# Reading the moving columns of two feed-forward projections in pieces, in a two-block transformer kernel

## The chip, the cores and the metric

The kernel runs on one core of a Trainium2 chip. The metric is device time in microseconds (us) of one execution. Inputs, weights and the output are in HBM; everything is float32.

## What is computed

Two transformer blocks over 512 tokens of width 1024. The change touches the feed-forward networks of the second block, which has two layers (`conv_ffn`, with `D_FF` = 2816):

```python
def causal_dwconv(u, w):
    width = w.shape[0]
    s = u.shape[1]
    up = jnp.pad(u, ((0, 0), (width - 1, 0), (0, 0)))
    return sum(up[:, i:i + s] * w[i] for i in range(width))

def conv_ffn(xn, w_up, conv_w, w_down):
    up = xn @ w_up
    a, g = jnp.split(up, 2, axis=-1)
    a = causal_dwconv(a, conv_w)
    return (jax.nn.silu(a) * g) @ w_down
```

and in `second_block`, for both layers: `xn = rmsnorm(x, ffn_norm[l])`, `x = x + conv_ffn(xn, ffn_w_up[l], ffn_conv[l], ffn_w_down[l])`. The first block has a network of the same shape with GELU. So there are three gate-and-value projections (`xn @ w_up`, 1024 to 5632 features): `up0` in the first block, `up1` and `up2` in the second.

## The kernel before

The activations lie transposed: 128 features on the partitions, 512 tokens along the free dimension, so a width of 1024 is a tile of 8 blocks of [128, 512]. Every linear layer is cut into *units*: a unit is one block of 128 output features over all (up to 8) input blocks, with a weight tile of 128 x 1024. A projection `up` has 44 units, taken in turn from the gate and the value half.

Products are made in two parts for precision. Each operand is split in a high part in float32r (WH, XH) and the rest (WL, XL); a unit's result is WH·XH + WH·XL + WL·XH, summed in one PSUM bank of [128, 512]. So each input block of a unit costs three matmuls with 512 moving columns (L1305, L1306, L1307 in the function `unit`), and a unit of 8 blocks 24. The moving operand is the activation, `xh[:, k0 + k, 0:width]`; the stationary operand is the weight.

Five engines work as a pipeline over the units, through semaphores, in the order in which the loops are written:
- SP brings a unit's weights to RAW, one of NSLOT = 4 slots (512 KB a unit).
- ACT makes WH from RAW (L501), POOL makes WL as RAW - WH in four pieces (L413).
- PE runs `unit`: it waits for `lo_ready` (the weights) and, in its caller, for `lin_free` (the bank), and raises `unit_done` at the end. Two banks, LB[0] and LB[1], are used in turn.
- DVE reads the bank: in `up` it multiplies it with the norm's factor R (L1121 for the gate half, L1126 for the value half), makes the convolution (L831, L839) and the product (L1130), which become the moving tiles FH and FL of the next projection, `down`.

On PE a stage is written as `linear(name, iters, per, ...)`: the first iteration by `body(0, True)`, the others in a loop on the engine. The very first unit of a stage is a call of its own, since it waits block by block for XH and XL; behind it stands the matmul that sums the squares for the norm (L1317, `norm`). The remaining 43 units of `up1` or `up2` go through the other branch of `body`. The stages follow one another: out, up0, down0, ain, aout, up1, down1, then attention, bout, up2, down2.

The line at which DVE evicts the banks of the first block's attention, L819 in `read_lin`, comes up in the prediction: for most units the output is written in one run, for those of the neighbourhood attention (KN) the output goes through `t.rearrange("p (c r) -> p r c", c=GRID)` with GRID = 64, so each element is written 8 elements from the one before.

Of the kernel before, what the change touches and what calls it, by code (L numbers as in the profile page):

```python
# [20 lines left out]
KB = D // P  # L21
S = 512
# [94 lines left out]
U, O = {}, {}  # L117
# [18 lines left out]
def two_blocks(nc, A, out):  # L136
# [4 lines left out]
    def fixed(name, shape, dt=F32):  # L141
        t = nc.alloc_sbuf_tensor_at(name, shape, dt, offset=top[0])
        n = 4
        for d in shape[1:]:
            n *= d
        top[0] += (n + 31) // 32 * 32
        return t
# [5 lines left out]
    WH = fixed("WH", [P, NSLOT, UW], F32R)  # L153
    WL = fixed("WL", [P, NSLOT, UW], F32R)
# [84 lines left out]
    LB = bank[0:2]  # L239
# [1050 lines left out]
    def _(pe):  # L1290
        mm = nc.tensor.matmul

        def unit(u0, j, i, per, kc, xh, xl, k0, dst, start=True, stop=True, width=S, ready=None, halfway=None):


            s = (u0 + j) % NSLOT
            pe.wait_ge(lo_ready, i * per + (u0 + j + 1))
            for k in range(kc):
                if halfway and k == kc // 2:
                    halfway()  # L1300
                if ready:
                    pe.wait_ge(ready[0], ready[1] + k + 1)
                w = slice(k * P, (k + 1) * P)
                a, b = xh[:, k0 + k, 0:width], xl[:, k0 + k, 0:width]
                mm(dst[:, 0:width], WH[:, s, w], a, start=start and k == 0, stop=False)  # L1305
                mm(dst[:, 0:width], WH[:, s, w], b, start=False, stop=False)  # L1306
                last = mm(dst[:, 0:width], WL[:, s, w], a, start=False, stop=stop and k == kc - 1)  # L1307
            last.then_inc(unit_done, 1)

        def norm(name, src, width, total):  # L1310

            pe.wait_ge(split_ready, total)
            if NORM[name]:
                pe.wait_ge(r_ready, NORM[name])
            if name == "down0":
                mm(bank[6][:], ONES[:], TC[:], start=True, stop=True).then_inc(fin_sum, 1)
            mm(NB[:, 0:width], ONES[:], src, start=True, stop=True).then_inc(norm_sum, 1)  # L1317
# [50 lines left out]
        for t, (un, st) in enumerate(SLOTS):  # L1368
            before = SLOTS[t - 1][1] if t else None
            if st and st[0] in ("xa", "na"):  # L1370
                kind, p, s = st
# [3 lines left out]
                for j in range(2):  # L1375
# [6 lines left out]
                    else:  # L1382
                        r = slice(64 * j, 64 * j + 64)
                        mm(SB[j][:, 0:M], QN[r, p % 2, P * s:P * (s + 1)], KN[r, p % 2, KEY0[s]:KEY0[s] + M],
                           start=True, stop=True)\
                            .then_inc(s_full, 1)
            if st and st[0] == "ml":
                _, h, s = st
# [13 lines left out]
            if un:  # L1402
                o = LEV[un]
                pe.wait_ge(lin_free, o + 1)
                if un[0] in ("memk", "memv"):
                    unit(0, UIDX[un], 0, 0, KB, MH, ML, 0, LB[o % 2], width=M,
                         ready=(split_ready, SPL["mem"]) if t == 0 else None)
                elif un[0] == "br":
                    unit(0, UIDX[un], 0, 0, 4, YH, YL, 4 * un[1], LB[o % 2], ready=(yl_ready, 4 * un[1]))
                else:  # L1410
                    unit(0, UIDX[un], 0, 0, KB, XH, XL, 0, LB[o % 2],
                         ready=(split_ready, SPL["x"]) if un == ("xq", 0) else None)
                if t == 0:
                    norm("mem", TD[:, 0:M], M, SPL["mem"] + KB)
                if un == ("xq", 0):
                    norm("x", SS[:], S, SPL["x"] + KB)
            for e in EXTRA[t]:
                o = LEV[e]
                pe.wait_ge(lin_free, o + 1)
                if e[0] == "hn":  # L1420
                    pe.wait_ge(h_sq, e[1] + 1)
                    last = mm(LB[o % 2][:], ONES[:], SQ[:], start=True, stop=True)
                elif e[1] == "gate":
                    pe.wait_ge(v_src, VSRC[e[1:]] + 1)
                    for k in range(TB):
                        last = nc.tensor.transpose(LB[o % 2][:, 64 * k:64 * k + 64], GT[:, 3, P * k:P * (k + 1)],
                                                   IDN[0:64, 0:64])
                else:
# [3 lines left out]
                    for k in range({"memv": MB, "nav64": TB - 1}.get(e[1], TB)):  # L1432
                        last = nc.tensor.transpose(LB[o % 2][:, P * k:P * (k + 1)],
                                                   TC[:, c0 + P * k:c0 + P * (k + 1)], IDN[:])
                last.then_inc(extra_full, 1)
            if st and st[0] in ("xa", "na"):
                for j in range(2):
# [3 lines left out]
                    for k in range(MB):  # L1441
                        last = nc.tensor.transpose(TRB[j][:, P * k:P * (k + 1)], SX[:, j, P * k:P * (k + 1)], IDN[:])
# [18 lines left out]
        def linear(name, iters, per, xh, xl, ready, norm_of=None, halfway=None):  # L1461


            def body(i, first):
                for j in range(per):
                    pe.wait_ge(lin_free, i * per + (O[name] + j + 1))
                    if first and j == 0:
                        unit(U[name], j, i, per, KB, xh, xl, 0, LB[O[name] % 2], ready=ready,
                             halfway=halfway)
                        if norm_of:  # L1470
                            norm(norm_of, SS[:], S, SPL[norm_of] + KB)
                    else:
                        unit(U[name], j, i, per, KB, xh, xl, 0, LB[(O[name] + j) % 2])

            body(0, True)
            with pe.Fori(1, iters) as i:
                body(i, False)
# [193 lines left out]
```

## Time and profile before

| | |
|---|---|
| median of 2 runs | 2271.99 us (2270.18 to 2273.8) |
| the profiled execution | 2267.01 us |
| its span, first to last instruction | 2265.3 us |
| mean granted TensorE clock | 0.989 |
| PE busy | 2174.4 us (96%) |
| weight loads on PE (beside the matmuls) | 1744.3 us (77%) |
| DVE, ACT, POOL busy | 1059.3, 871.6, 1175.9 us |
| moved by DMA | 204.92 MB, 90 GB/s |

The engines: PE is TensorE's matmuls and PEld its weight loads, DVE is VectorE, ACT ScalarE, POOL GpSimd, SP SyncE. Matmuls overlap one another and their recorded ends are modelled, so the pace of a row of matmuls is read from their starts. A clock of 1.00 is 2.4 GHz, 0.50 is 1.2 GHz. "Idle before" is the time that an engine stood still ahead of a group's instructions, with what ended it.

### The profile page before, as it was taken

What the parts mean: (1) busy time and instruction counts of PE and PEld (TensorE: products, weight loads), DVE (VectorE), ACT (ScalarE), POOL (GpSimd) and SP (SyncE); (2) the same over time, 40 slices, a digit from 0 to 9 for tenths busy, and PEclk for the clock granted to TensorE, in tenths of its full rate; (3) what the DMA queues carried; (4) which work ended last, traced back from release to release, by engine and by line L of the source; (5) the groups of instructions that cost most, each with busy time, mean ns of one, the idle gap of its engine ahead of it and who ended that gap; (6) DMA issues with size and microseconds to landing.
All of it is one profiled execution on the core that took longest, in us unless ns stands there. A gap on an engine that the chain in (4) does not pass through costs nothing.

```text
span 2265.3 us, 31096 instructions
## 1 busy us (share of the span) xinstructions
PE 2174.4 (96%) x9968; PEld 1744.3 (77%) x9968; DVE 1059.3 (47%) x1870; ACT 871.6 (38%) x1270; POOL 1175.9 (52%) x1572
## 2 busy tenths in 40 slices
PE   6999999799999999999999999998999989999999
PEld 5777666588888888888788888886677768888887
DVE  5466677533345543123435555115667664545400
ACT  6344223433344433232244443234444444443421
POOL 7443322777655555645456556654333325655653
PEclk9999999899999999999999999999999999999999
DMA  6213411233322233323223322332222202232332
GB/s 221 80 47 107 121 48 32 69 94 93 113 92 98 97 101 95 93 93 102 93 84 102 102 93 88 102 102 79 76 75 65 82 30 93 93 102 95 95 101 71
DMA packets 61469, 204.92 MB, mean 90 GB/s; under 512 B 6848, under 2 KB 6976, under 8 KB 61392
## 3 DMA queue, kind: packets, MB, share of 16 engines
q1 hardware_dynamic: 61200, 203.65, 28.1%
q8 instruction: 43, 0.70, 0.1%
q10 hardware_dynamic: 192, 0.30, 0.1%
q14 instruction: 34, 0.28, 0.0%
HBM read 201.52 MB, written 2.39 MB: 90 GB/s over the span
## 4 chain that ended last, share of the span: by engine, by line
PE 81%; DVE 8%; DVEq 4%; ACT 3%; issue 2%; POOL 1%; DMA 1%; ACTq 0%; SPq 0%
PE bank L1305 26%; PE bank L1307 26%; PE bank L1306 25%; PE bank L1513 1%; DVEq L1225 1%; DVE FX L1216 1%; PE bank L1567 1%; PE bank L1346 1%; DVE FX L1207 0%; DVE SS L1227 0%; DVEq L1231 0%; POOL YL L469 0%; DMA RAW<-in_w_att 0%; POOL WL L413 0%; ACT TD L729 0%
## 5 line engine op out<-in xcount | busy, mean ns | idle before, releaser
L413 POOL TENSOR_TENSOR WL<-RAW,WH 128x256 fp32r<-128x256 f32 x1496 | 1147.2, 800 | 1057.1 <-ACT WH L501 1056.9
L1305 PE MATMUL bank<-XH,WH 128*128 128x512 f32 x1840 | 730.2, 397 | 2.8 <-DVE XQ L821 2.0
L1307 PE MATMUL bank<-XH,WL 128*128 128x512 f32 x1840 | 716.7, 390 | 0.0
L1306 PE MATMUL bank<-XL,WH 128*128 128x512 f32 x1840 | 716.3, 389 | 0.0
L501 ACT ACTIVATE WH<-RAW 128x1024 fp32r<-128x1024 f32 x374 | 392.1, 1051 | 225.8 <-PE bank L1307 213.6
L1305 PEld LDWEIGHTS bank<-XH,WH 128*128 128x128 f32 x1840 | 345.4, 188 | 81.8 <-issue 6.6
L1306 PEld LDWEIGHTS bank<-XL,WH 128*128 128x128 f32 x1840 | 345.5, 188 | 76.3 <-issue 5.0
L1307 PEld LDWEIGHTS bank<-XH,WL 128*128 128x128 f32 x1840 | 345.4, 188 | 72.7
L1305 PE MATMUL bank<-FH,WH 128*128 128x512 f32 x528 | 208.0, 394 | 0.0
L1307 PE MATMUL bank<-FH,WL 128*128 128x512 f32 x528 | 207.0, 392 | 0.0
L1306 PE MATMUL bank<-FL,WH 128*128 128x512 f32 x528 | 204.9, 388 | 0.0
L1103 DVE TENSOR_TENSOR X<-X,bank 128x512 f32 x48 | 33.1, 689 | 322.2 <-PE bank L1307 322.2
L681 ACT ACTIVATE TD<-TC 128x512 f32<-128x512 f32 x66 | 41.8, 633 | 283.5 <-DVE TC L839 190.3
L839 DVE SCALAR_TENSOR_TENSOR TC<-TA,PAR,TC 128x511 f32<-128x511 f32 (+1 forms) x134 | 109.2, 815 | 22.3 <-issue 21.7
L1307 PEld LDWEIGHTS bank<-FH,WL 128*128 128x128 f32 x528 | 99.1, 188 | 23.2
L1306 PEld LDWEIGHTS bank<-FL,WH 128*128 128x128 f32 x528 | 99.1, 188 | 22.2
L1305 PEld LDWEIGHTS bank<-FH,WH 128*128 128x128 f32 x528 | 99.3, 188 | 19.7
L1121 DVE TENSOR_TENSOR TA<-bank,R 128x512 f32<-128x512 f32 x66 | 45.6, 692 | 134.1 <-PE bank L1307 121.6
L1305 PE MATMUL bank<-AH,WH 128*128 128x512 f32 x256 | 106.2, 415 | 1.6 <-DVE AL L1155 1.6
L1306 PE MATMUL bank<-AL,WH 128*128 128x512 f32 x256 | 101.3, 396 | 0.0
L1307 PE MATMUL bank<-AH,WL 128*128 128x512 f32 x256 | 101.1, 395 | 0.0
L1126 DVE TENSOR_TENSOR TE<-bank,R 128x512 f32<-128x512 f32 x66 | 45.6, 692 | 110.6 <-PE bank L1307 110.6
(276 smaller groups left out, 2342.1 us busy)
## 6 DMA issues: line engine op xcount, KB each, us to landing
RAW<-in_w_up SPq DMA_DIRECT2D x132, 512.0 KB, 3.5
RAW<-in_w_att SPq DMA_DIRECT2D x47, 512.0 KB, 3.6
RAW<-in_w_down SPq DMA_DIRECT2D x48, 448.0 KB, 3.3
RAW<-in_w_fa SPq DMA_DIRECT2D x32, 512.0 KB, 3.5
RAW<-in_w_down SPq DMA_DIRECT2D x24, 512.0 KB, 3.5
RAW<-in_w_ain SPq DMA_DIRECT2D x24, 512.0 KB, 3.5
RAW<-in_w_mrg SPq DMA_DIRECT2D x18, 512.0 KB, 3.6
RAW<-in_w_mrg SPq DMA_DIRECT2D x22, 256.0 KB, 2.7
```

The lines of the kernel that those rows point to most:

```text
L413: last = nc.gpsimd.tensor_tensor(WL[:, s, w], RAW[:, s, w], WH[:, s, w].bitcast(F32), ALU.subtract)
L501: A_(WH[:, s, :], RAW[:, s, :], ACT.Copy).then_inc(hi_ready, 1)
L681: A_(TD[:], TC[:], fn).then_inc(glu_ready, 1)
L839: last = v.scalar_tensor_tensor(out=TC[:, -d:S], in0=c[:, 0:S + d], scalar=w[k], in1=TC[:, -d:S], op0=ALU.mult, op1=ALU.add)
L1103: v.tensor_tensor(blk(X, nn), blk(X, nn), LB[(O[name] + n) % 2][:], ALU.add).then_inc(lin_free, 1)
L1121: v.tensor_tensor(TA[:], LB[0 if (O[name] % 2) == 0 else 1][:], R[:], ALU.mult)\
L1126: v.tensor_tensor(TE[:], LB[1 if (O[name] % 2) == 0 else 0][:], R[:], ALU.mult)\
L1216: v.tensor_scalar(FX[:, j, 0:nk], FX[:, j, 0:nk], RI[:, j:j + 1], None, ALU.mult)\
L1225: dve.drain().then_inc(q_ms, 1)
L1305: mm(dst[:, 0:width], WH[:, s, w], a, start=start and k == 0, stop=False)
L1306: mm(dst[:, 0:width], WH[:, s, w], b, start=False, stop=False)
L1307: last = mm(dst[:, 0:width], WL[:, s, w], a, start=False, stop=stop and k == kc - 1)
```

## The change

`unit` gets an argument `ways`. Where it is over 1, the moving operand (both its parts) and the output are seen through the same rearrangement `"p (v c e) -> p c v e"` with `v = ways` and `e = ways // 2`: the 512 columns are cut into `ways` places of 512 / ways columns, and the engine takes `e` columns from each place in turn. For `up1` (ways 4) these are pieces of 2 columns from 4 places 128 columns apart; for `up2` (ways 8) pieces of 4 columns from 8 places 64 columns apart. Input and output go through the same order, so each output column stands where it stood. The number of columns, the weights and all the waits are the same. All other stages, `up0` among them, call `unit` without it, and so does the first unit of each stage.

```diff
-        def unit(u0, j, i, per, kc, xh, xl, k0, dst, start=True, stop=True, width=S, ready=None, halfway=None):
+        def unit(u0, j, i, per, kc, xh, xl, k0, dst, start=True, stop=True, width=S, ready=None, halfway=None, ways=1):
...
                 a, b = xh[:, k0 + k, 0:width], xl[:, k0 + k, 0:width]
-                mm(dst[:, 0:width], WH[:, s, w], a, start=start and k == 0, stop=False)
-                mm(dst[:, 0:width], WH[:, s, w], b, start=False, stop=False)
-                last = mm(dst[:, 0:width], WL[:, s, w], a, start=False, stop=stop and k == kc - 1)
+                o = dst[:, 0:width]
+                if ways > 1:
+                    a, b, o = (t.rearrange("p (v c e) -> p c v e", v=ways, e=ways // 2) for t in (a, b, o))
+                mm(o, WH[:, s, w], a, start=start and k == 0, stop=False)
+                mm(o, WH[:, s, w], b, start=False, stop=False)
+                last = mm(o, WL[:, s, w], a, start=False, stop=stop and k == kc - 1)
             last.then_inc(unit_done, 1)
...
                     else:
-                        unit(U[name], j, i, per, KB, xh, xl, 0, LB[(O[name] + j) % 2])
+                        unit(U[name], j, i, per, KB, xh, xl, 0, LB[(O[name] + j) % 2],
+                             ways={"up1": 4, "up2": 8}.get(name, 1))
```

The order of the instructions on PE where `up1` passes from its first unit to the others, before:

```order
L1307 MATMUL bank<-XH,WL 128x512
L1317 MATMUL bank<-SS,ONES 128x512
L1305 MATMUL bank<-XH,WH 128x512
L1306 MATMUL bank<-XL,WH 128x512
L1307 MATMUL bank<-XH,WL 128x512
```

and with the change (its lines are numbered 3 higher from here on):

```order
L1310 MATMUL bank<-XH,WL 128x512
L1320 MATMUL bank<-SS,ONES 128x512
L1308 MATMUL bank<-XH,WH 128x64x4x2
L1309 MATMUL bank<-XL,WH 128x64x4x2
L1310 MATMUL bank<-XH,WL 128x64x4x2
```

Behind the norm's matmul every matmul of `up1` has the moving shape 64 x 4 x 2; none has moved. The same place in `up2`, with the change:

```order
L1310 MATMUL bank<-XH,WL 128x512
L1320 MATMUL bank<-SS,ONES 128x512
L1308 MATMUL bank<-XH,WH 128x16x8x4
L1309 MATMUL bank<-XL,WH 128x16x8x4
L1310 MATMUL bank<-XH,WL 128x16x8x4
```

There the shape is 16 x 8 x 4, and again no instruction stands elsewhere than before.

## Rows read from the trace of the kernel before

**Rows 1.** The page: busy time by engine, and TensorE's granted clock in 40 slices
```profile
PE 2174.4 (96%) x9968; PEld 1744.3 (77%) x9968; DVE 1059.3 (47%) x1870; ACT 871.6 (38%) x1270; POOL 1175.9 (52%) x1572
...
PEclk9999999899999999999999999999999999999999
```
**Rows 2.** The page: the chain that ended last, by engine and line
```profile
PE 81%; DVE 8%; DVEq 4%; ACT 3%; issue 2%; POOL 1%; DMA 1%; ACTq 0%; SPq 0%
PE bank L1305 26%; PE bank L1307 26%; PE bank L1306 25%; PE bank L1513 1%; DVEq L1225 1%; DVE FX L1216 1%; PE bank L1567 1%; PE bank L1346 1%; DVE FX L1207 0%; DVE SS L1227 0%; DVEq L1231 0%; POOL YL L469 0%; DMA RAW<-in_w_att 0%; POOL WL L413 0%; ACT TD L729 0%
```
**Rows 3.** Busy time by stretch: `up0`, `up1`, `up2`
```profile
core 0: us, PE busy (x) PEld busy (x) DVE busy (x) ACT busy (x) POOL busy (x), PEclk, DMA share, GB/s
637.30:871.40 234.10, 234.10 (x1033) 193.66 (x1032) 119.01 (x151) 99.64 (x111) 137.12 (x172) 1.00 0.29 95
1177.20:1411.30 234.10, 234.10 (x1033) 193.65 (x1032) 119.72 (x151) 99.69 (x111) 139.41 (x172) 1.00 0.30 95
...
1906.60:2140.70 234.10, 234.10 (x1033) 193.66 (x1032) 119.61 (x151) 99.68 (x111) 139.42 (x172) 1.00 0.29 95
```
**Rows 4.** Groups in `up1`: count, busy us, mean ns, idle before and releaser
```profile
L413 POOL TENSOR_TENSOR WL<-RAW,WH 128x256 fp32r<-128x256 f32 x172 | 139.4, 844 | 95.8 <-ACT WH L501 95.8
L1305 PE MATMUL bank<-XH,WH 128*128 128x512 f32 x344 | 134.2, 390 | 0.0
L1306 PE MATMUL bank<-XL,WH 128*128 128x512 f32 x344 | 133.8, 389 | 0.0
L1307 PE MATMUL bank<-XH,WL 128*128 128x512 f32 x343 | 133.4, 389 | 0.0
...
L1121 DVE TENSOR_TENSOR TA<-bank,R 128x512 f32<-128x512 f32 x22 | 15.2, 692 | 45.3 <-PE bank L1307 41.1 <-ACT R L521 4.2
L1126 DVE TENSOR_TENSOR TE<-bank,R 128x512 f32<-128x512 f32 x21 | 14.5, 692 | 34.6 <-PE bank L1307 34.6
```
**Rows 5.** Timeline of PE (start us, us): first and last matmuls of `up1`
```profile
1177.18 0.80 PE L1305 MATMUL bank<-XH,WH 128*128 128x512 f32 x1
...
1411.32 0.39 PE L1307 MATMUL bank<-XH,WL 128*128 128x512 f32 x1
1411.55 0.40 PE L1305 MATMUL bank<-FH,WH 128*128 128x512 f32 x1
```
**Rows 6.** Timeline of PE, matmuls of 256 columns in two stretches
```profile
22.75 0.28 PE L1306 MATMUL bank<-ML,WH 128*128 128x256 f32 x1
...
24.22 0.28 PE L1307 MATMUL bank<-MH,WL 128*128 128x256 f32 x1
27.53 0.41 PE L1305 MATMUL bank<-MH,WH 128*128 128x256 f32 x1 [3.03 <-POOL WL L413]
...
30.73 0.41 PE L1305 MATMUL bank<-MH,WH 128*128 128x256 f32 x1
```
**Rows 7.** Busy time by stretch, columns as in rows 3: these two stretches
```profile
22.70:24.30 1.60, 1.60 (x16) 1.60 (x15) 1.60 (x2) 1.60 (x4) 1.27 (x2) 1.00 0.66 266
27.50:30.70 3.20, 3.17 (x15) 3.20 (x16) 2.97 (x4) 2.60 (x5) 3.20 (x4) 0.53 0.51 164
```
**Rows 8.** Timeline of PE, moving tiles GH and GL
```profile
626.00 0.40 PE L1306 MATMUL bank<-GL,WH 128*128 128x512 f32 x1
...
628.10 0.40 PE L1306 MATMUL bank<-GL,WH 128*128 128x512 f32 x1
```
**Rows 9.** Line L819 on DVE: duration ns min/median/max
```profile
L819 DVE TENSOR_TENSOR TA<-bank,R x19: 627/682/692, 107.5 to 412.4; 128x512 f32<-128x512 f32 x19
...
L819 DVE TENSOR_TENSOR MK<-bank,RM x4: 424/424/426, 19.5 to 32.8; 128x256 f32<-128x256 f32 x4
...
L819 DVE TENSOR_TENSOR KN<-bank,R x4: 1086/1088/1100, 92.2 to 189.4; 128x512 f32<-128x512 f32 x4
```

## The prediction

> **What bounds the kernel now.** I read the page first: TensorE is busy 96% of the span and its granted clock stands in the top tenth in all 40 slices [rows 1]. The chain of work that ended last says the same of the path: 77% of the span are the three matmul lines of `unit` [rows 2]. Then I cut the stretches that the change touches out of the run. The gate-and-value projections are three stretches of 234.10 us each; in each, PE is busy for all of it, the clock is 1.00, DVE is busy 119 to 120 us, ACT under 100 and POOL under 140 [rows 3]. So in these stretches PE waits for nobody. The groups of the second stretch show it from the other side: the matmul rows have no idle time before them, while POOL waits 95.8 us for ACT, and DVE 41.1 and 34.6 us for PE [rows 4]. Whatever a matmul there takes longer goes to the end of the kernel one for one.
>
> The duration in a matmul's row (389 to 390 ns) is no cost, since matmuls overlap and their ends are modelled. The cost is the distance from start to start. The second stretch starts with the matmul at 1177.18, and the next projection's first starts at 1411.55 [rows 5]: 234.37 us for 43 units of 24 matmuls (344 of each of the three lines [rows 4], one record is missing), that is 1032 matmuls and 227.1 ns each.
>
> Is 227.1 ns limited by the array or by the reading of the moving columns? Early in the run there are matmuls of 256 columns at both levels of the clock. At 2.4 GHz 13 of them take 24.22 - 22.75 = 1.47 us, 113.1 ns each; at 1.2 GHz 15 of them take 30.73 - 27.53 = 3.20 us, 213.3 ns each [rows 6]. The clock of the two stretches reads 1.00 and 0.53, the latter because its end is already fast [rows 7]. 213.3 ns is 256 / 1.2 to the digit. Half of it would be 106.7, and 113.1 is 6% more; 227.1 is 6% over 512 / 2.4 = 213.3 as well. So at the high clock something beside the array sets the pace, and it goes with the number of columns. The tile that is read matters too: with GH and GL as moving operand, nine matmuls take 628.10 - 626.00 = 2.10 us, 233 ns each, at the same shape [rows 8]. I read this as the reading side running without reserve: it delivers one column in 0.444 ns and no more. That is the point of the profile that speaks for a cost of a less convenient order of reading.
>
> **The change part by part.** No instruction is added, removed or moved, and no wait. Two groups of matmuls get another order of columns, for both the moving operand and the PSUM output. The first unit of each stage keeps the old form, so 43 units of 24, 1032 matmuls, change in the second projection and 1032 in the third. In the second the engine makes 256 jumps a matmul (512 columns in pieces of 2), in the third 128 jumps (pieces of 4). Weight loads, DMAs, ACT, POOL and DVE work keep their sizes; they have slack in these stretches [rows 3] and more of it if PE slows.
>
> What a jump costs on TensorE no row shows: every matmul of the kernel before reads and writes its columns in one run. The nearest rows are of DVE [rows 9]. One line evicts a bank of 512 elements: TA in 682 ns in one run, KN in 1088 ns, where the output steps by 8 elements each time. The same line takes 424 ns for 256 elements in one run. So an element in a run costs (682 - 424) / 256 = 1.01 ns, the 512 jumps add 406 / 512 = 0.79 ns each, and a place that is left after each access takes 1.80 ns in all. It is another engine, and a write, so it is an estimate for TensorE.
>
> How it carries over has three answers. First: 1.80 ns is a floor from one place to the next and streaming hides below it. A piece of 2 streams in 2 x 0.444 = 0.89 ns, so the floor decides: 256 x 1.80 = 461 ns, 234 ns more than 227.1. A piece of 4 streams in 1.77 ns, practically the floor: 128 x 1.80 = 230.4, 3.3 ns more. The sum: 1032 x 0.234 = 241.5 us for the second projection and 1032 x 0.0033 = 3.4 us for the third, against the profiled execution's 2267.0 us (span 2265.3): 2267.0 + 241.5 + 3.4 = 2511.9, rounded 2512 us. With 1.77 ns as the floor it would be 2267 + 234 = 2501. Second: all of it is hidden and the sum is zero. Third: each jump adds its 0.79 ns unhidden. The bounds for one matmul are then: below, 213.3 ns (nothing passes the array's own pace, so at best -13.8 ns); above, the 461 of the floor for pieces of 2, and for pieces of 4 the pace of the low clock, 426.7. I take the first answer, because the reading side is at its limit already in one run [rows 6] and the one measured jump is longer than a piece of 2 lasts. The median of the runs shown, 2271.99, lies 5 us over the profiled execution; the forecast against it would be 2517.
>
> The rows say that a jump costs DVE 0.79 ns where one stands after every element [rows 9]. The Trainium skill, page "Vector Engine (DVE) Microarchitecture Reference", section "Measured stream behaviour on trn2", says that runs of two adjacent words on an 8-byte boundary keep the full rate with any hop between them, and its figures for one jump per element (1.71 to 1.76 ns) agree with the 1.80 here. Taken over to TensorE as it stands it would make both changed stages free, 2267 us; DVE takes a pair in two of its slow steps, though, and TensorE in 0.89 ns. That is why I don't let this rule decide.
>
> **The rivals.** *A, nothing changes.* Pairs are enough for the reading side and for PSUM at this pace, or neighbouring reads are fetched ahead in several places at once. For it: the 6% loss at the high clock may be another thing than reading of the moving columns, such as the weight loads that run beside them, and then there may be reserve. Against it: the 233 ns of the G tiles [rows 8] show the pace to hang on which tile is read. Time: 2267 + 0, at most 2064 x 0.006 = 12 us more if the new order hits what the G tiles hit. This is the case on the other side of my forecast; it decides if a piece of 2 is delivered within 0.89 ns after a jump. The Trainium skill, page "Advanced Engine Details and Errata", section "Memory Cachelines", gives a rule that also ends here: two accesses to one 16-byte line of SBUF absorb its latency, and in PSUM every two consecutive elements should be contiguous; no run here shows it yet.
>
> *B, both stages are slower.* Each jump costs, on the reading or on the writing side, and isn't hidden: 256 x 0.79 = 202 ns and 128 x 0.79 = 101 ns a matmul, 1032 x 0.303 = 313 us, 2580 us. At the upper bound (both at the low clock's pace, +199.6 ns on 2064 matmuls) it would be 2267 + 412 = 2679. For it: the accumulation in the bank takes the same jumps as the read, and the bank's places lie 128 and 64 columns apart; against it: nothing in the trace shows a write limit. The same section of the Trainium skill says first that any non-contiguous pattern in PSUM slows matmuls significantly, which would be this case.
>
> *C, faster.* The new order avoids what makes 227.1 of 213.3: at most 2064 x 13.8 ns = 28 us, 2239 us, 1.3%. Even this is no gain of 2%; for more the array would have to take columns faster than its clock.
>
> *D, the change does nothing.* The order of instructions shows both new shapes in the programs, so the patterns aren't merged back to one run; D would look like A.
>
> **How the numbers follow.** The likeliest case, pieces of 2 slowed to the floor and pieces of 4 free: 0.38, at 2512 us, its own range 2490 to 2530. A with D: 0.36, 2262 to 2280. B with all sizes between: 0.24, 2330 to 2680. C: 0.02. About 2% either way is what a measurement of this kernel can tell from no change. Faster by more than that needs what C excludes: 0.01. Within 2%: A, D, C and the small end of B, 0.37. Slower: 0.62. The range goes from A to the middle of B, 2262 to 2600; left out are the upper part of B, about 0.1, and a little under A.
>
> **What would show it.** Right: the stretch of the second projection at about 476 us with starts 461 ns apart, the third at 234 to 238 us with 227 to 231 ns, and the first, unchanged, at 234 us; DVE waiting longer for PE in the second only; clock still 1.00 there. If the clock read 0.50 there, the pace could not be under 427 ns whatever the reading does. Wrong: starts 227 ns apart in both (A), or over 300 ns in the third (B). The step most likely to fail is the transfer of the 1.80 ns from a DVE write to a TensorE read.

## The result and the profile after

The changed kernel takes 2548.66 us (median of 2 runs, 2547.95 to 2549.37), against 2271.99 before: a ratio of 1.1224, 95% interval 1.1206 to 1.1243. Its profiled execution took 2547.95 us, 280.9 more than that of before.

The page, busy time and clock, as in [rows 1]:

```profile
PE 2459.4 (97%) x9968; PEld 1774.5 (70%) x9968; DVE 1031.9 (41%) x1870; ACT 874.5 (34%) x1270; POOL 1142.1 (45%) x1572
...
PEclk9999998999999999999999999999999999999999
```

PE is busy 285 us longer with the same 9968 matmuls at the same clock. ACT has 3 us more to do, and DVE and POOL have less. The only other row that grows is PE's own weight loads, by 30 us. So PE was slowed, and nobody else.

Where the time went is seen in busy time by stretch, as in [rows 3], each stretch from the start of a stage's first matmul behind the norm's to the start of the next stage's first. (The counts take in matmuls that reach in at either end. `up0`, `up1`, `down1`, `up2`:)

```profile
638.61:872.98 234.37, 234.37 (x1035) 193.86 (x1033) 118.89 (x151) 99.76 (x111) 137.71 (x173) 1.00 0.29 95
...
1178.50:1636.39 457.89, 457.89 (x1035) 213.77 (x1033) 102.87 (x151) 99.76 (x111) 123.36 (x176) 1.00 0.15 50
1636.39:1759.62 123.23, 123.23 (x530) 99.81 (x528) 16.87 (x25) 33.94 (x39) 69.23 (x96) 1.00 0.31 93
2134.48:2421.86 287.38, 287.38 (x1034) 198.89 (x1033) 109.71 (x151) 102.59 (x111) 126.67 (x175) 1.00 0.24 78
```

`up0`, which isn't changed, has its 234.37 us. `up1` has 457.89, 223.5 more: 1032 matmuls, 443.7 ns from start to start instead of 227.1. `up2` has 287.38, 53.0 more, 278.5 ns each. `down1` behind the slowed stage has 123.23 instead of the 120.87 that it has in the kernel before; that makes 2.4. Together 278.9 of the 280.9 us.

`down1` is not changed, and yet its matmuls stand 233.4 ns apart instead of 228.9. The same happens to an unchanged `down` stage in runs 1, 7 and 8 below, always behind a slow stage, but not behind each. The kernel before has both paces within one stage too, its `out` projection, which reads the tiles GH and GL:

```profile
586.65 0.39 PE L1305 MATMUL bank<-GH,WH 128*128 128x512 f32 x1
...
591.00 0.39 PE L1306 MATMUL bank<-GL,WH 128*128 128x512 f32 x1
...
591.70 0.40 PE L1306 MATMUL bank<-GL,WH 128*128 128x512 f32 x1
...
631.13 0.40 PE L1307 MATMUL bank<-GH,WL 128*128 128x512 f32 x1
```

The first 19 take 4.35 us, 228.9 ns each, and from 591.70 on 169 take 39.43 us, 233.3 each. At the first pace the distances repeat in threes (226, 229 and 232 ns by the trace), at the second all are 233 or 234. So one and the same row of matmuls has two rhythms. What switches between them is open, and differences of some 5 ns between the stages below can't be told from it.

The groups in `up1`, as in [rows 4]:

```profile
L1308 PE MATMUL bank<-XH,WH 128*128 128x512 f32 x344 | 219.2, 637 | 0.0
L1309 PE MATMUL bank<-XL,WH 128*128 128x512 f32 x344 | 218.8, 636 | 0.0
...
L413 POOL TENSOR_TENSOR WL<-RAW,WH 128x256 fp32r<-128x256 f32 x176 | 123.4, 732 | 336.6 <-ACT WH L501 336.6
L1310 PEld LDWEIGHTS bank<-XH,WL 128*128 128x128 f32 x344 | 71.2, 207 | 81.3 <-issue 81.3
```

The matmuls still have no idle time before them: PE waits for no semaphore, it is slow inside the instruction. POOL's idle time rises from 95.8 to 336.6 us. The weight loads of one line, which had 13.5 us of idle time, have 81.3; one of them takes 207 ns instead of 188. DVE waits longer for PE, in `up1` and also in `up2` (one view of each stretch):

```profile
L1121 DVE TENSOR_TENSOR TA<-bank,R 128x512 f32<-128x512 f32 x22 | 15.2, 692 | 160.9 <-PE bank L1310 156.7 <-ACT R L521 4.2
...
L1121 DVE TENSOR_TENSOR TA<-bank,R 128x512 f32<-128x512 f32 x22 | 15.2, 692 | 71.4 <-PE bank L1310 67.2 <-ACT R L521 4.2
```

Before, it waited 41.1 us at this line in each of the two stages.

### The profile page after: what moved, and what is told of

It is laid out like the page before. It is cut to its first block, busy times and chain, and to the rows that moved or that the text cites. A ratio compares the mean times of both kernels' runs of the same rounds, so it can differ in the third digit from the quotient of the medians.

```text
span 2546.2 us, 31096 instructions
## 1 busy us (share of the span) xinstructions
PE 2459.4 (97%) x9968; PEld 1774.5 (70%) x9968; DVE 1031.9 (41%) x1870; ACT 874.5 (34%) x1270; POOL 1142.1 (45%) x1572
## 4 chain that ended last, share of the span: by engine, by line
PE 83%; DVE 7%; DVEq 3%; ACT 3%; issue 2%; POOL 1%; DMA 1%; SPq 0%; ACTq 0%
PE bank L1308 27%; PE bank L1310 26%; PE bank L1309 26%; PE bank L1517 1%; DVEq L1225 1%; DVE FX L1216 1%; PE bank L1349 0%; PE bank L1571 0%; DVE SS L1227 0%; DVEq L1231 0%; DVE FX L1207 0%; ACT TD L729 0%; ACT TD L727 0%; POOL YL L469 0%; DVEq L1190 0%
## 5 line engine op out<-in xcount | busy, mean ns | idle before, releaser
L413 POOL TENSOR_TENSOR WL<-RAW,WH 128x256 fp32r<-128x256 f32 x1496 | 1113.4, 777 | 1371.7 <-ACT WH L501 1371.6
L1308 PE MATMUL bank<-XH,WH 128*128 128x512 f32 x1840 | 836.2, 454 | 2.8 <-DVE XQ L821 2.0
L1310 PE MATMUL bank<-XH,WL 128*128 128x512 f32 x1840 | 821.8, 447 | 0.0
L1309 PE MATMUL bank<-XL,WH 128*128 128x512 f32 x1840 | 821.7, 447 | 0.0
L1308 PEld LDWEIGHTS bank<-XH,WH 128*128 128x128 f32 x1840 | 354.8, 193 | 166.1 <-issue 88.7
L1309 PEld LDWEIGHTS bank<-XL,WH 128*128 128x128 f32 x1840 | 354.7, 193 | 160.2 <-issue 86.3
L1310 PEld LDWEIGHTS bank<-XH,WL 128*128 128x128 f32 x1840 | 354.5, 193 | 157.3 <-issue 81.3
L1121 DVE TENSOR_TENSOR TA<-bank,R 128x512 f32<-128x512 f32 x66 | 45.7, 692 | 276.4 <-PE bank L1310 263.7
L684 ACT ACTIVATE FH<-TA 128x512 f32 x66 | 42.3, 641 | 283.2 <-DVE TA L1130 283.2
L839 DVE SCALAR_TENSOR_TENSOR TC<-TA,PAR,TC 128x511 f32<-128x511 f32 (+1 forms) x134 | 103.6, 773 | 22.4 <-issue 21.7
```

The source lines that it names most:

```text
L413: last = nc.gpsimd.tensor_tensor(WL[:, s, w], RAW[:, s, w], WH[:, s, w].bitcast(F32), ALU.subtract)
L684: A_(blk(FH, i * 2 + n), TA[:], ACT.Copy).then_inc(ffh_ready, 1)
L839: last = v.scalar_tensor_tensor(out=TC[:, -d:S], in0=c[:, 0:S + d], scalar=w[k], in1=TC[:, -d:S], op0=ALU.mult, op1=ALU.add)
L1121: v.tensor_tensor(TA[:], LB[0 if (O[name] % 2) == 0 else 1][:], R[:], ALU.mult)\
L1308: mm(o, WH[:, s, w], a, start=start and k == 0, stop=False)
L1309: mm(o, WH[:, s, w], b, start=False, stop=False)
```

## The experiments

All twelve are made from the kernel of before. `unit` gets a form of three values: the number of places, the columns in a piece, and the sides that take this order (r the moving operand, w the output). The table names the stages:

```diff
+                o = dst[:, 0:width]
+                if form:
+                    v, e, side = form
+                    view = lambda t: t.rearrange("p (v c e) -> p c v e", v=v, e=e)
+                    if "r" in side:
+                        a, b = view(a), view(b)
+                    if "w" in side:
+                        o = view(o)
```

Each run has up to six stages in other forms, and each stage is read by itself: its length from start to start over 1032 matmuls (`up`) or 528 (`down`). In one run, `up` stages take 227.1 ns a matmul and `down` stages 228.9 (or 233.4). Where one run only was taken, the text goes by this pace, which came out at 234.37 to 234.38 us in every unchanged `up` stage, and not by the total. The theory on record is the forecast's: the reading side needs a least time for each place that it comes to. The main rival is the bank's side.

**1. Only the moving operand in pieces.**

```diff
+FORM = {'up1': (4, 2, 'r'), 'up2': (8, 4, 'r')}
```

> Only the moving operand is read in pieces; the output is written in one run, so the columns land permuted. Theory R (the reading side sets the pace): the starts stay as with the change, 443.7 ns apart in the second projection and 278.5 in the third, about 2549 us. Theory W (writing to the bank sets it): 227 ns in both, about 2270 us. Theory M (each side costs on its own): between, each stage losing part.

Measured: 2552.48 us. `up1` and `up2` by stretch:

```profile
1183.05:1640.93 457.88, 457.88 (x1034) 213.77 (x1033) 102.86 (x151) 99.74 (x111) 123.33 (x176) 1.00 0.15 50
...
2139.03:2426.41 287.38, 287.38 (x1035) 198.88 (x1033) 109.75 (x151) 102.66 (x111) 126.63 (x175) 1.00 0.24 78
```

The same 457.88 and 287.38 us as with the whole change.

**2. Only the output in pieces.**

```diff
+FORM = {'up1': (4, 2, 'w'), 'up2': (8, 4, 'w')}
```

> Only the output is written in pieces; the moving operand is read in one run, so the columns land permuted. Theory R: 227 ns in both stages, about 2270 us. Theory W: 443.7 and 278.5 ns, about 2549 us. The third projection lost 51 ns a matmul where the floor of 1.73 ns a piece (443.7 / 256) hidden below streaming gives nothing; a mixed theory has these 51 ns come from the write and the 216 of the second from the read: then 227 and 278 here, about 2325 us.

Measured: 2271.66 us, beside 2272.03 of before on the same chip.

```profile
1180.46:1414.84 234.38, 234.38 (x1035) 193.87 (x1034) 119.69 (x151) 99.78 (x111) 139.51 (x173) 1.00 0.30 95
1414.84:1535.70 120.86, 120.86 (x529) 99.16 (x528) 17.23 (x25) 33.93 (x39) 72.53 (x100) 1.00 0.33 98
1911.23:2145.60 234.37, 234.37 (x1034) 193.92 (x1033) 119.64 (x151) 99.78 (x111) 139.51 (x173) 1.00 0.29 95
```

Not a nanosecond. Theory R holds in both stages, W and the mixed theory fall: the 51 ns of `up2` are the reading's too, so the floor alone doesn't explain them.

**3. Other sizes and places.**

```diff
+FORM = {'up0': (4, 4, 'rw'), 'up1': (8, 2, 'rw'), 'up2': (4, 8, 'rw'), 'down0': (4, 16, 'rw'), 'down1': (4, 32, 'rw'), 'down2': (8, 8, 'rw')}
```

> Other sizes and places, read and written alike, outputs in place: up0 pieces of 4 from 4 places, up1 pieces of 2 from 8, up2 pieces of 8 from 4, down0 pieces of 16 from 4, down1 pieces of 32 from 4, down2 pieces of 8 from 8. Theory size (cost by the number of jumps, whatever the distance): up0 278, up1 444, up2 and down2 between 227 and 253 (64 jumps at 0.40 ns each are 26), down0 +13, down1 +6 over 228.9. Theory distance (the number of places or their distance counts): up0 and up1 differ from the 278.5 and 443.7 of the changed kernel by over 10 ns. Theory floor (a piece costs the greater of 1.73 ns and its streaming): up2 and the down stages unchanged at 227 and 229.

Measured: 2601.43 us; 268.4, 487.0 and 231.5 ns in the `up` stages, 236.6, 233.4 and 241.8 in the `down` stages. `up0` and `up1`:

```profile
642.01:918.98 276.97, 276.97 (x1035) 201.59 (x1033) 111.66 (x151) 101.13 (x111) 126.25 (x174) 1.00 0.25 81
...
1228.58:1731.18 502.60, 502.60 (x1035) 215.83 (x1033) 102.87 (x151) 100.44 (x111) 124.07 (x176) 1.00 0.14 45
```

Pieces of 4 from 4 places cost 10 ns less than from 8, pieces of 2 from 8 places 43 ns more than from 4. The number of jumps is the same in each pair, so the number alone doesn't set the cost. Neither does the plain floor: `down2` is 13 ns over 228.9.

**4. Near and far places.**

```diff
+FORM = {'up0': (2, 2, 'rw'), 'up1': (128, 2, 'rw'), 'up2': (2, 4, 'rw'), 'down0': (64, 4, 'rw'), 'down1': (64, 2, 'rw'), 'down2': (2, 16, 'rw')}
```

> Near and far places, read and written alike, outputs in place: up0 pieces of 2 from 2 places 256 columns apart, up1 pieces of 2 from 128 places 4 columns apart, up2 pieces of 4 from 2 places 256 apart, down0 pieces of 4 from 64 places 8 apart, down1 pieces of 2 from 64 places 8 apart, down2 pieces of 16 from 2 places. Theory jump (any jump costs the same): 444, 444, 278, 280, 446 and about 242 ns. Theory memory (what costs is which stretch of memory is touched next; words already fetched are kept): up0 and up1 are much under 444, as each stretch of 4 columns is used twice soon or the next one lies beside it.

Measured: 2762.98 us; 328.7, 451.5 and 250.4 ns, and 233.3, 461.1 and 240.0 ns. `up0`, `down0` and `up1`:

```profile
641.43:980.66 339.23, 339.23 (x1035) 202.43 (x1033) 104.50 (x151) 99.53 (x111) 123.25 (x176) 1.00 0.21 66
980.66:1103.86 123.20, 123.20 (x529) 98.93 (x528) 24.91 (x33) 38.17 (x46) 71.07 (x97) 1.00 0.32 96
...
1288.51:1754.44 465.93, 465.93 (x1035) 214.48 (x1033) 102.88 (x151) 99.57 (x111) 125.30 (x176) 1.00 0.15 49
```

Pieces of 4 in steps of 8 columns take 233.3 ns, no more than a `down` stage takes at times by itself, though each of 128 pieces is jumped to: a jump as such costs next to nothing. Pieces of 2 in steps of 4 columns cost 451.5 although the next piece lies close by. `up0` shows something kept: with two places each stretch of 4 columns is used again at the next access but one, and this takes 328.7 ns, not 444. The memory theory was right on that and wrong on `up1`.

**5. Pieces of 4 from 4 places at odd distances.** Here and in runs 6, 9 and 10 the places are laid over the neighbouring block of XH too, so that their distance is free; other columns are read than the sum needs.

```diff
+FORM = {'up0': ('at', 4, 132, 4, 0), 'up1': ('at', 4, 136, 4, 0), 'up2': ('at', 4, 144, 4, 0)}
...
+                if form and form[0] == "at":
+                    _, v, dist, e, off = form
+                    c0 = S * min(k0 + k, KB - 2) + off
+                    t = S // v
+
+                    def view(x):
+                        x = x[:].rearrange("p k s -> p (k s)")[:, c0:c0 + v * dist]
+                        x = x.rearrange("p (v x) -> p v x", v=v)[:, :, 0:t]
+                        return x.rearrange("p v (c e) -> p c v e", e=e)
+
+                    a, b = view(xh), view(xl)
```

> Read only, pieces of 4 from 4 places, whose distance is 132 columns in up0, 136 in up1 and 144 in up2, where the sizes run had 128 and 268.4 ns (other columns are read than the sum needs, the number of columns is the same). Theory bank (a place that is a multiple of 32 columns away lies in the same part of the memory as the last one and must wait for it): 132 and 136 are free, 227 to 233 ns, and 144 is free or part of the cost. Theory jump (every far place costs 0.3 to 0.4 ns): 268 in all three.

Measured: 2279.11 us; 231.5, 233.7 and 227.1 ns.

```profile
637.35:876.28 238.93, 238.93 (x1035) 193.92 (x1033) 120.74 (x151) 99.70 (x111) 137.83 (x173) 1.00 0.29 93
...
1181.83:1423.03 241.20, 241.20 (x1034) 193.15 (x1033) 122.38 (x151) 99.58 (x111) 133.29 (x173) 1.00 0.28 92
...
1918.75:2153.08 234.33, 234.33 (x1035) 194.18 (x1034) 119.25 (x151) 99.73 (x111) 134.21 (x173) 1.00 0.29 95
```

268.4 ns at a distance of 128 columns, 227.1 at 144 with the same number of equally far jumps. The distance is what costs, as the bank theory has it. (Pieces of 4 laid over in this way at 128 columns, beginning on a stretch of 4, were not run; in run 10 pieces of 2 laid over at 260 columns take the same 328.7 ns as in place at 256 in run 4, so the laying over by itself costs nothing there.)

**6. Alignment.**

```diff
+FORM = {'up0': ('at', 4, 128, 4, 2), 'up1': ('at', 1, 512, 512, 2), 'up2': ('at', 4, 132, 2, 0)}
```

> Read only. up0: pieces of 4 from 4 places 128 apart, as in the sizes run (268.4 ns), but each begins 2 columns (8 bytes) later. up1: one run of 512 that begins 2 columns later. up2: pieces of 2 from 4 places 132 apart. Theory line (memory is read in stretches of 4 columns, 16 bytes, each costing about 1.73 ns when it is come to): up0 pays for two stretches a piece, about 450 to 500 ns, up1 is unchanged at 227, up2 stays near 444. Theory word (pairs are the unit): up0 stays at 268. With the bank theory on top up2 falls from 444 to that part which no neighbouring place explains, 328 to 444.

Measured: 2735.38 us; 447.0, 232.9 and 453.7 ns.

```profile
638.19:1099.52 461.33, 461.33 (x1035) 217.89 (x1033) 104.07 (x151) 99.61 (x111) 123.13 (x176) 1.00 0.15 49
...
1405.05:1645.40 240.35, 240.35 (x1034) 195.32 (x1033) 117.45 (x151) 99.69 (x111) 139.01 (x173) 1.00 0.29 93
```

Pieces of 4 that begin 8 bytes later cost as much as pieces of 2: each touches two aligned stretches of 4 columns, 256 stretches a matmul, 1.75 ns each. So the unit is the aligned stretch of 16 bytes, and what is paid is its visits. One run of 512 that begins in the middle of a stretch costs 5.8 ns, which I had expected to be free. Pieces of 2 gained nothing from leaving the distance of 128 (453.7 at 132, 10 ns more than at 128): the bank theory's lower time did not come. The Trainium skill ("Advanced Engine Details and Errata", section "Memory Cachelines") gives lines of 16 bytes in SBUF; this agrees. It also says that two hits on a line absorb the latency; for float32 columns at TensorE's high clock they don't: pieces of 2 take 443.7 instead of 227.1 ns.

**7. The low clock, and near distances.**

```diff
+FORM = {'up0': (32, 4, 'rw'), 'up1': (16, 4, 'rw'), 'up2': (32, 2, 'rw')}
...
-                    unit(0, UIDX[un], 0, 0, KB, MH, ML, 0, LB[o % 2], width=M,
+                    unit(0, UIDX[un], 0, 0, KB, MH, ML, 0, LB[o % 2], width=M, form=(4, 2, "rw"),
```

> The early matmuls of 256 columns (memory's key and value) read in pieces of 2 from 4 places 64 apart; they run at either level of the clock. up0: pieces of 4 from 32 places 16 apart; up1: pieces of 4 from 16 places 32 apart; up2: pieces of 2 from 32 places 16 apart. Theory floor (the memory has a time of its own of 1.7 to 1.9 ns a piece): 220 to 245 ns at both levels, against 113 and 213.3 in one run. Theory cycles (the cost goes with TensorE's clock): near 225 ns at 2.4 GHz and 440 at 1.2. Theory bank: up0 and up1 show from which distance on pieces of 4 cost (233 at 8 columns, 278 at 64); theory jump: both 278. up2 about 450.

Measured: 2516.57 us; 227.0, 247.0 and 431.5 ns in the `up` stages. The early matmuls of 256 columns, timeline of PE:

```profile
14.12 0.40 PE L1316 MATMUL bank<-ML,WH 128*128 128x256 f32 x1
14.35 0.40 PE L1317 MATMUL bank<-MH,WL 128*128 128x256 f32 x1
...
17.29 0.40 PE L1315 MATMUL bank<-MH,WH 128*128 128x256 f32 x1
...
30.54 0.42 PE L1315 MATMUL bank<-MH,WH 128*128 128x256 f32 x1
...
32.11 0.42 PE L1316 MATMUL bank<-ML,WH 128*128 128x256 f32 x1
```

The second stretch by its clock, and a weight load in each of the two:

```profile
30.54:32.11 1.57, 1.57 (x8) 1.45 (x7) 1.46 (x2) 1.57 (x3) 1.57 (x2) 1.00 0.20 68
...
14.12 0.31 PEld L1317 LDWEIGHTS bank<-MH,WL 128*128 128x128 f32 x1
...
30.55 0.21 PEld L1316 LDWEIGHTS bank<-ML,WH 128*128 128x128 f32 x1
```

From 14.12 to 17.29 are 14 matmuls, 226.4 ns each; from 30.54 to 32.11 are 7, 224.3 each. In the kernel before, the same early matmuls ran 213.3 ns apart:

```profile
13.35 0.41 PE L1306 MATMUL bank<-ML,WH 128*128 128x256 f32 x1
...
17.18 0.40 PE L1306 MATMUL bank<-ML,WH 128*128 128x256 f32 x1
```

(18 of them in 3.84 us by the trace; the rows are rounded). That is the pace of 1.2 GHz. The profile has no clock record of these first microseconds, in either kernel. The weight loads tell the level in its place: in the kernel before they take 0.33 us there and in the stretch recorded at 1.2 GHz (27.7 to 31.1 us), and 0.19 at 2.4 GHz; here they take 0.31 in the first stretch and 0.21 in the second. At the low pace, then, pieces of 2 cost 13 ns, at the high one (113.1 ns in one run, [rows 6]) 111 ns, and both end at 128 visits of 1.75 to 1.77 ns. The floor is one in nanoseconds and not in TensorE's cycles; theory cycles falls. The distances: 227.0 ns at 16 columns, 247.0 at 32, the latter from `up1`:

```profile
1190.95:1445.90 254.95, 254.95 (x1035) 199.01 (x1033) 110.64 (x151) 99.77 (x111) 134.37 (x174) 1.00 0.26 87
```

**8. Only the second projection.**

```diff
+FORM = {'up1': (4, 2, 'rw')}
```

> Only the second projection reads and writes in pieces (2 from 4 places); the third is as before. If the two parts add: 2272 + 1032 x 0.2166 = 2272 + 223.5, plus 2.4 for the projection behind it, 2498 us. If part of the cost comes from an interplay of the two, or goes elsewhere, it differs by over 5 us.

Measured: 2497.73 us (median of 4 runs, 2496.92 to 2499.46), against 2270.81 (median of 7) of before on the same chip: ratio 1.1003, interval 1.0984 to 1.1021. `up1`, `down1` and `up2`:

```profile
1180.97:1638.86 457.89, 457.89 (x1035) 213.77 (x1033) 102.85 (x151) 99.74 (x111) 123.33 (x176) 1.00 0.15 50
1638.86:1762.09 123.23, 123.23 (x530) 99.81 (x529) 16.87 (x25) 33.94 (x39) 69.24 (x96) 1.00 0.30 93
2136.49:2370.86 234.37, 234.37 (x1034) 193.86 (x1033) 119.92 (x151) 99.77 (x111) 137.75 (x173) 1.00 0.29 95
```

The parts add: 2498 expected, 2497.73 measured, and the 51 us up to the 2548.66 of the whole change are `up2`.

**9. Pieces of 4 from 8 places, as in `up2`, at other distances.**

```diff
+FORM = {'up0': ('at', 8, 68, 4, 0), 'up1': ('at', 8, 72, 4, 0), 'up2': ('at', 8, 80, 4, 0)}
```

> Read only, pieces of 4 from 8 places as in the changed third projection (278.5 ns at a distance of 64 columns), but 68 columns apart in up0, 72 in up1 and 80 in up2. Theory bank: the 51 ns of the changed kernel come from the distance alone, so all three fall to 227 to 234 ns, and the kernel takes about 2280 us. Theory number (more places cost more, whatever the distance): 278 in all three, about 2430 us.

Measured: 2280.20 us; 230.4, 233.0 and 224.8 ns.

```profile
641.24:879.03 237.79, 237.79 (x1034) 193.97 (x1033) 115.53 (x151) 99.70 (x111) 134.90 (x173) 1.00 0.29 94
...
1184.53:1424.98 240.45, 240.45 (x1035) 194.02 (x1033) 117.55 (x151) 99.71 (x111) 138.73 (x173) 1.00 0.29 93
...
1922.09:2154.11 232.02, 232.02 (x1034) 193.39 (x1033) 121.22 (x151) 99.66 (x111) 136.63 (x173) 1.00 0.30 96
```

The 51 ns of the changed `up2` are gone with the distance of 64 columns, down to a rest of -2 to 6 ns. So the distance is their cause; why the distance costs is not shown.

**10. Pieces of 2 at other distances.**

```diff
+FORM = {'up0': ('at', 2, 260, 2, 0), 'up1': ('at', 8, 72, 2, 0), 'up2': ('at', 4, 144, 2, 0)}
```

> Read only, pieces of 2: up0 from 2 places 260 columns apart, up1 from 8 places 72 apart, up2 from 4 places 144 apart. Theory line with bank: each visit of a stretch of 4 columns costs 1.73 to 1.8 ns, so up1 falls from 487 (64 apart) to 444 to 461 and up2 is 444 to 454. up0 tells whether the stretch last read is kept: if so it stays at or under the 328.7 of the near-places run; if what made 328.7 was the distance of 256, it goes to 450.

Measured: 2839.17 us; 328.7, 461.7 and 440.4 ns. `up0`, `up1` and `up2`:

```profile
640.38:979.60 339.22, 339.22 (x1034) 202.69 (x1033) 104.39 (x151) 99.54 (x111) 123.15 (x176) 1.00 0.20 66
...
1285.14:1761.60 476.46, 476.46 (x1035) 216.04 (x1033) 102.77 (x151) 99.53 (x111) 122.86 (x176) 1.00 0.15 48
...
2258.64:2713.08 454.44, 454.44 (x1034) 214.48 (x1033) 102.78 (x151) 99.55 (x111) 123.48 (x176) 1.00 0.15 50
```

Of the surcharge of 8 places 64 apart (487.0, 43 ns over the 443.7 of 4 places) 25 ns go with the distance, 18 stay; the doubling stays too. And 328.7 ns at 260 columns as at 256: it looks as if something of the stretch before the last were kept, at either distance.

**11. Output in other pieces.**

```diff
+FORM = {'up0': (2, 2, 'w'), 'up1': (128, 2, 'w'), 'up2': (64, 4, 'w')}
```

> Write only: output in pieces of 2 from 2 places 256 apart in up0, of 2 from 128 places 4 apart in up1, of 4 from 64 places 8 apart in up2. Theory free write (pairs are enough for the bank, wherever they go): 227 ns in all three, about 2272 us. Theory hidden write cost (only these distances are slow): one of the stages is over 240 ns.

Measured: 2271.64 us, 234.37 us in each of the three stages. With run 2 that makes five orders of writing, none of which costs anything. The Trainium skill says in the section named above that any non-contiguous pattern in PSUM slows matmuls significantly, and also that every two consecutive elements should be contiguous; for pieces of 2 and 4 the runs contradict the first sentence and agree with the second. Pieces of 1 were not tried, so that pairs are needed is not shown.

**12. Larger pieces.**

```diff
+FORM = {'up0': (32, 8, 'rw'), 'up1': (16, 8, 'rw'), 'up2': (8, 16, 'rw'), 'down0': (32, 4, 'rw'), 'down1': (32, 8, 'rw'), 'down2': (16, 16, 'rw')}
```

> Larger pieces, read and written alike, outputs in place: up0 pieces of 8 from 32 places 16 columns apart, up1 of 8 from 16 places 32 apart, up2 of 16 from 8 places 64 apart, down0 of 4 from 32 places 16 apart, down1 of 8 from 32 places, down2 of 16 from 16 places. Theory bank (only a step between stretches that meets a busy part costs; half or a quarter as many far steps as with pieces of 4): up1 about 227 + 10 = 237, up2 about 227 + 13 = 240 ns, the others 227 and 229. If an order of reading can beat one run, it is up0 or down0, which may fall under 227.1 and 228.9 as the distance of 80 did (224.8); theory none: nothing in place is under 226.5.

Measured: 2293.25 us; 233.7, 220.5 and 239.9 ns, and 233.3, 235.6 and 240.0 ns. `up1`:

```profile
1186.81:1414.32 227.51, 227.51 (x1034) 193.50 (x1033) 125.33 (x151) 99.50 (x111) 142.06 (x172) 1.00 0.30 98
```

The pieces of 8 and 16 in `up2` and `down2` (64 and 32 columns apart) cost 11 to 13 ns, `up2` as the bank theory has it; the pieces 16 columns apart (`up0`, `down0`, `down1`) cost 4 to 7 and gained nothing. `up1` surprised: pieces of 8 from 16 places 32 columns apart take 220.5 ns, 6.6 less than one run, where I had expected 237. So an order of reading can also gain, and the bank theory in my simple form (far steps cost, near ones don't) is incomplete. It was seen in one stage of one run. If it held for the three `up` stages it would be 3 x 1032 x 6.6 ns = 20 us, 0.9%; a kernel with this form in all of them was not tried, and whether the place of the tiles or of the weights has a part in it is open.

## Why the prediction came out

The total came out inside the range, 2547.95 us in 2262 to 2600, and the step named as the most likely to fail, the 1.80 ns of a place, held within 4%. But it lies outside the likeliest case's own range of 2490 to 2530. The wide range took it in, and two errors of opposite sign helped: that the total fits so well is in part luck.

**What bounds it.** Right. Each nanosecond added to a matmul of the two stages went to the end: 276.5 of the 280.9 us lie in them, with no engine's wait in between. (A small misreading: the clock in [rows 1] stands in the top tenth in 39 of the 40 slices, and is 8 in one; the changed stretches have 1.00.)

**The side and the mechanism.** Right: the cost is on the reading side (runs 1 and 2), a place that is come to has a least time, and this time is independent of TensorE's clock (run 7). It was put as a floor "from one place to the next"; run 6 makes it sharper: a floor for each aligned stretch of 4 columns that is visited. That the reading sets the pace even in one run is borne out by run 12, where another order alone gives 220.5 instead of 227.1 ns. That all 13.8 ns above 213.3 are the reading's is inferred, from 128 visits of 1.77 ns beside the 1.73 of the pieces of 2; the weight loads that run beside were not varied. One support of the prediction was misread: the 233 ns with GH and GL were taken to show that the tile matters. The same stage begins at 228.9 ns on the same tiles, and FH and FL have both paces, so the 233 ns are a rhythm and not the tile's.

**The term for pieces of 2.** 256 x 1.80 ns, taken over from a write of DVE, was 461 ns; measured 443.7, so 1.73 ns a visit and 223.5 us instead of 241.5. That an estimate from another engine came within 4% may be luck: no run shows that DVE's writes and TensorE's reads have this time from the same cause. One element per jump on DVE and two on TensorE can pay the same only because both stream in less (1.01 and 0.89 ns). It is this whole slow step of 1.80 ns that is longer than a piece of 2 lasts, and not, as the prediction has it, the jump alone: that is 0.79.

**The term for pieces of 4.** This step failed in size: 3.4 us were forecast, 53.0 measured. The floor's share was right (128 visits at 1.73 to 1.77 ns are 221 to 227 ns, the pace of one run; run 9 has 224.8 to 233.0 ns). What I hadn't priced is that the distance of the places matters: 64 columns cost 51 ns a matmul, 128 cost 41, 256 cost 23, 32 cost 20, and 8, 16, 68, 72, 80, 132, 136 and 144 cost between -2 and 7. Against the profiled execution's 2547.95 us the forecast of 2511.9 is 36 us low: 50 too little here, 18 too much in the other term, and 2.4 of `down1` and 2.0 outside these stages that it didn't have.

**The rivals.** A (nothing changes) fell: its point of decision, a piece of 2 delivered within 0.89 ns after a jump, is missed by a factor of two. The rule for VectorE that the prediction weighed and set aside (Trainium skill, "Vector Engine (DVE) Microarchitecture Reference", section "Measured stream behaviour on trn2": pairs keep the full rate) doesn't carry over to TensorE, which uses up a pair in half the floor's time. The figures of that section which the prediction found to agree with its 1.80 ns are mostly those for hops of 4 KiB; for a write in steps of 24 words the Trainium skill has 2.50 ns in the same table, so the agreement is looser than it was put. B named a cost in both stages, and by the total its 2580 us is no worse than the 2512 that was put first: 32 us too high against 36 too low. Its 202 ns for pieces of 2 also comes near the 216.6 measured. What rules it out is that its unhidden 0.79 ns a jump would be 101 ns for pieces of 4 at any distance, where 128 jumps cost 51 in `up2` and -2 to 7 at eight other distances (runs 4, 5, 7 and 9); and writing has no part. B's upper end took 426.7 ns for pieces of 2 as well, less than the 461 of the prediction's own bounds, and less than the 443.7 measured. Of C (the order of reading saves what makes 227.1 of 213.3) there is nothing in this change, but run 12 shows that it is no empty case: 220.5 ns.

**What was to be seen.** `up0` unchanged and the clock at 1.00, as put. `up1` at 457.9 us instead of the 476 named and `up2` at 287.4 instead of 234 to 238, off by the terms above. `up2`'s starts, 278.5 ns apart, are neither the 227 to 231 that was to show it right nor the over 300 of B. And DVE was to wait longer for PE in `up1` only; it did so in `up2` too (67.2 us at L1121 instead of 41.1), as `up2` was slower than forecast.

## What to carry to other kernels

For float32r operands at TensorE's high clock the moving columns should be read in aligned stretches of 4 (16 bytes): half a stretch, or a piece of 4 that begins 8 bytes late, nearly doubles the matmul at this clock (443.7 and 447.0 ns instead of 227.1). Where a layout asks for jumps, whole stretches are nearly free, unless the places lie 32, 64, 128 or 256 columns apart (seen with pieces of 4); put another distance than these between them. Larger pieces at such distances went both ways, 220.5 to 241.8 ns, so they have to be measured. Reorder on the output side if there is a choice: in pieces of 2 and 4 it cost nothing. And read a stage's pace from the starts of its matmuls, since the durations shown (390 and 637 ns) are not the cost; a difference of 5 ns between stages can be one of rhythm.

## What was not expected of the hardware

- One float32r run of 512 columns is itself, as far as these runs tell, held by the reading: 227.1 ns against 213.3 at the array's pace. That is 1.77 ns for each stretch of 4 columns, and visits that use half of one cost about as much, 1.69 to 1.90 ns (431.5 to 487.0 ns over 256). At 1.2 GHz the same reading is hidden (213.3 ns for 256 columns).
- The same matmuls in one run have two rhythms, 228.9 and 233.4 ns, on the same tiles and in one case within one stage. What switches between them is open.
- With pieces of 4, distances of 32, 64, 128 and 256 columns cost up to 0.4 ns a visit (51.4 ns over 128 visits); 16, 80 and 144, odd multiples of 16, cost nothing in the `up` stages. How the memory is divided that this comes out is open.
- With pieces of 2 from two places, where each stretch is used again at the next access but one, a matmul takes 328.7 ns instead of 440 to 487.
- The order with 8 columns from 16 places ran faster than one run, 220.5 ns.
